# A two-layer block kernel: the second layer's middle norm taken from three sums, the residual added in pieces, and two transposed groups instead of six ahead of a product

## The chip, the cores and the metric

The kernel runs on one core of one Trainium2 chip. The metric is the device time of one execution in microseconds (us). Engines in the profile: PE is TensorE's matmul queue and PEld its weight loads, DVE is VectorE, ACT is ScalarE, POOL is GpSimd, SP is SyncE, which issues the weight transfers.

## What is computed

Two transformer layers over 256 tokens of width 2048. Only the second one matters here; in it the change touches the two places where an RMS norm stands ahead of a weight product. Cut to that:

```python
def rms_norm_2(x, g):
    y = x * lax.rsqrt(jnp.mean(x * x, axis=-1, keepdims=True) + EPS)
    return y * g

h = modulate(rms_norm_2(x, pre_norm_mix), shift_m, scale_m)   # first norm: ahead of w_in
...                                                           # attention on h @ w_in
o = jnp.concatenate([o_n, o_m], axis=-1) @ w_o
x = x + gate_m[:, None, :] * rms_norm_2(o, post_norm_mix)
h = modulate(rms_norm_2(x, pre_norm_ffn), shift_f, scale_f)   # middle norm: ahead of w_up
f = jnp.square(jax.nn.relu(h @ w_up)) @ w_down
```

Write g for `o * gate_m * post_norm gain` and r for the reciprocal root of the mean square of `o`. Then the new x is x + r g, and its mean square is mean(x²) + r (2 mean(x g) + r mean(g²)). That identity is what the changed kernel uses.

## The kernel before

Every weight product runs as a *phase* of *units*. A unit is a 512-row by 512-column piece of a weight matrix (`w_in2a` uses 432 columns); it is handled as two halves, and a half is 12 matmuls on PE: two blocks of 128 rows (kt), two blocks of 128 tokens (h), and three products each (high x high, high x low, low x high), since every fp32 operand is split in a high part and a remainder. A phase has two column blocks b of four units u; column block b accumulates in the PSUM banks `GP[:, 2b..2b+1]`. For each half ACT makes the high part (`whi`, `split_hi`) and DVE the remainder (`wlo`, `split_lo`) in a ring of four halves. `w_oa`, `w_ob` and some others also carry four *ada* units (DVE only, `ada_acc`), a matrix-vector product that makes the modulation vectors.

The left operand of a product behind a norm (`hhi`, `hlo`, transposed to 16 blocks of 128 features by 256 tokens) is made in eight groups g of two blocks. For one group: x times 1/rms goes into `xn` (`second_scale` on DVE for columns 0 to 511, `second_scaled(i, k)` on ACT for the later quarters k), PE transposes it (`second_turn`, eight matmuls on two groups, line 841), DVE applies gain and shift into one of two buffers `flat` (`second_full`, two instructions), ACT copies that to the high part (`second_upper`), DVE subtracts for the low part (`second_lower`, which releases semaphore `norm_lo`). Half (u, s) of column block 0 needs group 2u+s, and PE waits for it by `norm_lo`. i = 0 is the first norm, i = 1 the middle one. All queues are in program order; each engine's order is written out by hand, and *hooks* put small work behind a given unit of a phase, `{5: [...]}` behind the fifth unit.

Between `w_ob` and `up20`, in the kernel before: `post_mean` and `post_root` give r; DVE adds `x += r * g` in eight pieces of 512 columns (`post_add`, line 2231); ACT squares seven of them for the new mean square (line 1724), DVE the eighth (line 2250); a root; a reciprocal; then the scaling and the groups. PE transposes groups 0 to 5 ahead of the product, groups 6 and 7 behind its unit 0.

In `w_oa`, four small products `gate_row` on PE (line 1275) spread the gate vector over the partitions. They form a loop over engines: DVE makes a diagonal tile `dg` (line 2211) behind the two `wlo` of a unit, PE multiplies it behind the next unit, ACT copies the result (line 1682) and then makes the two `whi` of the next unit:

```python
phase(PH["w_oa"], joined(store(PH["w_oa"], o2), {3 + i: [lambda it, i=i: gate_copy(0, i)] for i in range(4)},
                         {7: [lambda it: post_block(0, 0)]}))
```

## Time and profile before

| what | value |
| --- | --- |
| runs | 2827.8, 2829.64, 2836.27 us; median 2829.64 us |
| profiled execution | 2827.76 us, its span 2825.9 us |
| PE busy | 2746.7 us, 97% of the span |
| PE weight loads busy | 2346.6 us, 83% |
| DVE busy | 1785.4 us, 63% |
| ACT busy | 1314.4 us, 47% |
| mean granted TensorE clock | 0.989 of full |

Busy time is the time in which an engine executed something; idle time of PE is where time can be won or lost in this kernel, while idle time of DVE and ACT costs nothing unless PE waits for them. The span is counted from the first to the last instruction; the remaining 1.9 us of the profiled execution lie around it.

### The profile page before, as it was taken

What the parts mean: (1) busy time and instruction counts of PE and PEld (TensorE: products, weight loads), DVE (VectorE), ACT (ScalarE), POOL (GpSimd) and SP (SyncE); (2) the same over time, 40 slices, a digit from 0 to 9 for tenths busy, and PEclk for the clock granted to TensorE, in tenths of its full rate; (3) what the DMA queues carried; (4) which work ended last, traced back from release to release, by engine and by line L of the source; (5) the groups of instructions that cost most, each with busy time, mean ns of one, the idle gap of its engine ahead of it and who ended that gap; (6) DMA issues with size and microseconds to landing.
All of it is one profiled execution on the core that took longest, in us unless ns stands there. A gap on an engine that the chain in (4) does not pass through costs nothing.

```text
span 2825.9 us, 34968 instructions
## 1 busy us (share of the span) xinstructions
PE 2746.7 (97%) x13414; PEld 2346.6 (83%) x13414; DVE 1785.4 (63%) x2030; ACT 1314.4 (47%) x1656; POOL 170.3 (6%) x132
## 2 busy tenths in 40 slices
PE   8998999999999999999999999998989999999998
PEld 8998888888778888888888889887878888888886
DVE  4466668776558888865555564546675756644555
ACT  5554244454435545434454554446454444344453
POOL 0001630000000000000000000820000000000000
PEclk9999999999999999999999999999999999999999
DMA  8553038887647777876556556550655866755553
GB/s 281 161 175 122 0 143 288 288 278 268 224 163 257 281 276 272 284 252 208 184 179 209 188 183 198 198 172 16 225 192 182 282 220 225 266 188 181 188 188 119
DMA packets 293266, 579.60 MB, mean 205 GB/s; under 512 B 9168, under 2 KB 46192, under 8 KB 292112
## 3 DMA queue, kind: packets, MB, share of 16 engines
q1 hardware_dynamic: 291296, 566.08, 59.6%
q0 software_dynamic: 1120, 8.57, 0.8%
q10 hardware_dynamic: 720, 3.15, 0.3%
q8 instruction: 90, 1.47, 0.2%
q14 instruction: 40, 0.33, 0.0%
HBM read 575.66 MB, written 2.10 MB: 204 GB/s over the span
## 4 chain that ended last, share of the span: by engine, by line
PE 94%; DVE 3%; ACT 1%; issue 1%; DMA 0%; POOL 0%; SPq 0%; DVEq 0%; ACTq 0%
PE GP L866 28%; PE GP L868 28%; PE GP L867 28%; PE TA L841 2%; PE TB L841 1%; PE TB L489 1%; PE GP L466 1%; PE TA L1225 0%; DVE x L2231 0%; PE GP L1069 0%; PE TA L1069 0%; PE GP L1059 0%; DVE wlo L1794 0%; DMA x<-in_x 0%; PE TA L1275 0%
## 5 line engine op out<-in xcount | busy, mean ns | idle before, releaser
L1794 DVE TENSOR_TENSOR wlo<-raw,whi 128x1024 fp32r<-128x1024 f32 (+2 forms) x904 | 1085.3, 1214 | 813.3 <-ACT whi L1318 804.1
L1318 ACT CAST whi<-raw 128x1024 fp32r<-128x1024 f32 (+2 forms) x904 | 923.7, 1029 | 1172.3 <-PE GP L868 1115.4
L866 PE MATMUL GP<-whi,hhi 128*128 128x512 f32 (+2 forms) x1792 | 688.6, 384 | 2.9 <-issue 2.9
L868 PE MATMUL GP<-whi,hlo 128*128 128x512 f32 (+2 forms) x1792 | 680.5, 380 | 0.0
L867 PE MATMUL GP<-wlo,hhi 128*128 128x512 f32 (+2 forms) x1792 | 679.9, 379 | 0.0
L866 PEld LDWEIGHTS GP<-whi,hhi 128*128 128x128 f32 x1792 | 337.6, 188 | 53.6 <-issue 4.4
L868 PEld LDWEIGHTS GP<-whi,hlo 128*128 128x128 f32 x1792 | 337.3, 188 | 52.2
L867 PEld LDWEIGHTS GP<-wlo,hhi 128*128 128x128 f32 x1792 | 337.7, 188 | 50.6 <-issue 1.0
L866 PE MATMUL GP<-whi,bhi 128*128 128x512 f32 x704 | 276.7, 393 | 0.2 <-DVE blo L1855 0.2
L1782 DVE SCALAR_TENSOR_TENSOR ada_acc<-raw,csig,ada_acc 128x512 f32<-128x512 f32 x360 | 270.2, 751 | 10.2
L868 PE MATMUL GP<-whi,blo 128*128 128x512 f32 x704 | 274.3, 390 | 0.0
L867 PE MATMUL GP<-wlo,bhi 128*128 128x512 f32 x704 | 273.9, 389 | 0.0
L866 PE MATMUL GP<-whi,f2hi 128*128 128x512 f32 x512 | 201.4, 393 | 0.0
L868 PE MATMUL GP<-whi,f2lo 128*128 128x512 f32 x512 | 199.3, 389 | 0.0
L867 PE MATMUL GP<-wlo,f2hi 128*128 128x512 f32 x512 | 199.3, 389 | 0.0
L868 PEld LDWEIGHTS GP<-whi,blo 128*128 128x128 f32 x704 | 132.1, 188 | 27.8
L866 PEld LDWEIGHTS GP<-whi,bhi 128*128 128x128 f32 x704 | 132.2, 188 | 27.2 <-DVE blo L1855 0.7
L867 PEld LDWEIGHTS GP<-wlo,bhi 128*128 128x128 f32 x704 | 132.3, 188 | 26.5
L866 PE MATMUL GP<-whi,fhi 128*128 128x512 f32 x352 | 137.3, 390 | 0.0
L868 PE MATMUL GP<-whi,flo 128*128 128x512 f32 x352 | 137.0, 389 | 0.0
L867 PE MATMUL GP<-wlo,fhi 128*128 128x512 f32 x352 | 136.9, 389 | 0.0
L867 PEld LDWEIGHTS GP<-wlo,f2hi 128*128 128x128 f32 x512 | 96.1, 188 | 20.7 <-issue 1.0
(416 smaller groups left out, 2601.2 us busy)
## 6 DMA issues: line engine op xcount, KB each, us to landing
raw<-in_w_up SPq DMA_DIRECT2D x108, 1024.0 KB, 5.3
raw<-in_w_down SPq DMA_DIRECT2D x108, 1024.0 KB, 5.1
raw<-in_w_ada SPq DMA_DIRECT2D x96, 1024.0 KB, 5.2
raw<-in_w_gate SPq DMA_DIRECT2D x44, 1024.0 KB, 5.3
raw<-in_w_in SPq DMA_DIRECT2D x48, 856.0 KB, 4.7
raw<-in_w_xkv SPq DMA_DIRECT2D x32, 1024.0 KB, 5.6
raw<-in_w_in SPq DMA_DIRECT2D x24, 1024.0 KB, 5.0
raw<-in_w_in SPq DMA_DIRECT2D x24, 864.0 KB, 4.6
```

What stands on the lines that cost most here:

```text
L466: m = pe.matmul(o[:, h * T:h * T + u["L"]], l, r, start=(d == 0), stop=(d == n - 1), skip_group_check=True)
L489: m = pe.matmul(bank[:, j * P:j * P + P], l, r, start=(d == 0), stop=(d == len(terms) - 1), skip_group_check=True)
L841: return pe.transpose(dst, src, ident[0:n, 0:n] if n != P else ident)
L866: pe.matmul(o, ahi[:, kt, t], whi[r][:, k, 0:q.width], start=first, stop=False)
L867: pe.matmul(o, ahi[:, kt, t], wlo[r][:, k, 0:q.width], start=False, stop=False)
L868: m = pe.matmul(o, alo[:, kt, t], whi[r][:, k, 0:q.width], start=False, stop=last)
L1318: nc.scalar.copy(whi[(2 * g + s) % NRING][:, :, 0:q.width], raw[j % NSLOT][:, 2 * s:2 * s + 2, 0:q.width])\
L1782: m = nc.vector.scalar_tensor_tensor(ada_acc[:, :], raw[j % NSLOT][:, k, :], c, ada_acc[:, :], ALU.mult, ALU.add)
L1794: TTo(wlo[r][:, :, 0:q.width], raw[j % NSLOT][:, 2 * s:2 * s + 2, 0:q.width], whi[r][:, :, 0:q.width].bitcast(F32), ALU.subtract).then_inc ...
```

## The change

Five edits:

1. In both norms PE transposes only groups 0 and 1 ahead of the product; groups 2 and 3, 4 and 5, 6 and 7 are transposed in the middle of units 0, 1 and 2 (behind their first half). ACT and DVE take the groups in an order to match.
2. The mean square of the new x comes from three sums of four blocks each. ACT squares x in `w_oa` (`x_squares`, eight instructions) and g in `w_ob` and behind it (`gated_squares`, eight); DVE multiplies x and g (`crossed`, eight), of which two instructions stand in `w_oa`, four in `w_ob` and two behind it.
3. The squares of the new x are gone: seven on ACT, one on DVE.
4. `x += r * g` is done in pieces: two `post_add` ahead of the scaling, the other six each between `second_full` and `second_lower` of groups 0 to 5 (`mixed_pair`). ACT scales quarter k of the new x only after both of its pieces.
5. Of the first quarter's two scalings in the middle norm ACT takes one and DVE the other.

```diff
-            for g in range(6):
+            for g in range(2):
                 second_turn(0, g)
             product(PH["w_in2a"], hhi, hlo, None, first=lambda: None, halves=lambda u, s: (S("norm_lo"), 32 + 2 * u + s + 1),
-                    points={(0, 0, 0): lambda: (second_turn(0, 6), second_turn(0, 7))})
+                    points=second_turns(0))
...
+            def second_turns(i):
+                return {(0, 0, u, "half"): lambda u=u: (second_turn(i, 2 * u + 2), second_turn(i, 2 * u + 3)) for u in range(3)}
...
+            def x_squares(b):
+                for h in range(NH):
...
+                    nc.scalar.activation(fbx[1], x[:, h, 512 * b:512 * b + 512], ACT.Square, scale=D ** -0.5,
+                                         accum_out=xs[:, 4 * h + b:4 * h + b + 1]).then_inc(S("x_ss"), 1)
...
             phase(PH["w_oa"], joined(store(PH["w_oa"], o2), {3 + i: [lambda it, i=i: gate_copy(0, i)] for i in range(4)},
+                                     {3 + b: [lambda it, b=b: x_squares(b)] for b in range(4)},
                                      {7: [lambda it: post_block(0, 0)]}))
...
-            for i in range(7):
-                b, h = divmod(i, 2)
-                act.wait_ge(S("y_mix"), i + 1)
-                act.wait_ge(S("norm_ss"), 31 + i)
-                nc.scalar.activation(junk[0][:, :], x[:, h, 512 * b:512 * b + 512], ACT.Square,
...
-            second_uppers(1)
+            second_scaled(1, 0)
+            second_upper(1, 0)
+            second_upper(1, 1)
+            second_scaled(1, 1)
+            split_hi(PH["up20"], 0, 1)
+            second_upper(1, 2)
+            second_upper(1, 3)
+            second_scaled(1, 2)
...
+            def crossed(b, h):
+                link(nc.vector.scalar_tensor_tensor(junk[1][:, :], o2[:, h, 512 * b:512 * b + 512], 2.0 / D, x[:, h, 512 * b:512 * b + 512],
+                                                    ALU.mult, ALU.mult, accum_out=xs[:, 8 + 4 * h + b:9 + 4 * h + b]))
+
+            def gated_sums(b):
+                gated(0, b).then_inc(S("og"), 1)
+                dve.wait_ge(S("og"), b + 1)
+                for h in range(NH):
+                    crossed(b, h)
...
-            second_pair(1, 0)
+
+            def mixed_pair(b):
+                for h in range(NH):
+                    second_full(1, 2 * b - 2 + h)
+                    post_add(0, b, h, "y_mix")
+                    second_lower(1, 2 * b - 2 + h)
+
+            mixed_pair(1)
             split_lo(PH["up20"], 0, 1)
-            second_pair(1, 2)
-            second_pair(1, 4)
+            mixed_pair(2)
...
-                phase(PH[f"up2{s}"], hooks, head={3: [] if s else [lambda it: second_pair(1, 6)]})
+                phase(PH[f"up2{s}"], hooks, head={3: []} if s else {3: [lambda it: mixed_pair(3)], 4: [lambda it: second_pair(1, 6)]})
```

What stands on DVE behind the scaling of the middle norm, before. `flat<-TA` and its like are `second_full`, `hlo<-` is `second_lower`, `wlo<-` is `split_lo` of `up20`; the words in brackets are the semaphores that an instruction waits for.

```order
L2142 TENSOR_SCALAR flat<-TA,tab,shifts 128x256 [waits norm_lo,norm_t]
L2142 TENSOR_SCALAR flat<-TA,tab,shifts 128x256
L2142 TENSOR_SCALAR flat<-TA,tab,shifts 128x256 [waits norm_lo,norm_t]
L2142 TENSOR_SCALAR flat<-TA,tab,shifts 128x256
L2149 TENSOR_TENSOR hlo<-flat,hhi 128x512 [waits norm_hi] x2
L1794 TENSOR_TENSOR wlo_55<-raw,whi_51 128x1024 [waits hi_done]
L1794 TENSOR_TENSOR wlo_56<-raw,whi_52 128x1024 [waits hi_done]
L2142 TENSOR_SCALAR flat<-TB,tab,shifts 128x256 [waits norm_lo,norm_t]
```

The same place in the changed kernel, up to the same instruction; `x<-o` is `post_add`:

```order
L2173 TENSOR_SCALAR flat<-TA,tab,shifts 128x256 [waits norm_lo,norm_t]
L2173 TENSOR_SCALAR flat<-TA,tab,shifts 128x256
L2262 SCALAR_TENSOR_TENSOR x<-o_50_110,small,x 128x512
L2180 TENSOR_TENSOR hlo<-flat,hhi 128x512 [waits norm_hi]
L2173 TENSOR_SCALAR flat<-TA,tab,shifts 128x256 [waits norm_lo,norm_t]
L2173 TENSOR_SCALAR flat<-TA,tab,shifts 128x256
L2262 SCALAR_TENSOR_TENSOR x<-o_50_110,small,x 128x512
L2180 TENSOR_TENSOR hlo<-flat,hhi 128x512 [waits norm_hi]
L1825 TENSOR_TENSOR wlo_55<-raw,whi_51 128x1024 [waits hi_done]
L1825 TENSOR_TENSOR wlo_56<-raw,whi_52 128x1024 [waits hi_done]
L2173 TENSOR_SCALAR flat<-TB,tab,shifts 128x256 [waits norm_lo,norm_t]
```

Each group now carries one piece of the residual between its full values and its low part.

On ACT at the same place, in the changed kernel (`xn_p<-x` is `second_scaled`, `hhi<-flat` is `second_upper`, `whi<-raw` is `split_hi` of `up20`):

```order
L1630 CAST hhi<-flat 128x512 [waits norm_f] x2
L1625 ACTIVATE xn_p_113<-x,small 128x512 [waits y_mix]
L1625 ACTIVATE xn_p_113<-x,small 128x512
L1327 CAST whi_51<-raw 128x1024 [waits mm_done,raw_in1]
L1327 CAST whi_52<-raw 128x1024 [waits mm_done]
L1630 CAST hhi<-flat 128x512 [waits norm_f] x2
```

Before, quarters 1 and 2 were scaled ahead of all of this, and the two casts of `raw` stood directly behind the first two of `hhi`.

On ACT in `w_oa`, in the changed kernel, a stretch of the loop through `gate_row`; the row with `flat,small<-x` is new:

```order
L1690 COPY gpb_51_111<-TA 128x512 [waits gate_mm]
L1719 ACTIVATE flat,small<-x 128x512 [waits x_ss] x2
L1327 CAST whi_49<-raw 128x1024 [waits mm_done,raw_in2]
L1327 CAST whi_50<-raw 128x1024 [waits mm_done]
L1690 COPY gpb_51_111<-TA 128x512 [waits gate_mm]
```

The two squares stand between the copy of a gate row and the casts of the next unit; before, the casts followed the copy directly.

## Rows read from the trace of the kernel before

**Rows 1.** Whom PE waited for: us in total, times, longest us

```profile
PE TA L841 <- DVE xn_p L2132: 11.3, 1, 11.3
```

**Rows 2.** Timeline of PE, middle norm: start us, us, instruction [idle before <- releaser]

```profile
2089.18 1.97 PE L841 MATMUL TA<-cst,xn_p 128*128 128x128 f32 x8 [11.26 <-DVE xn_p L2132]
...
2094.05 0.48 PE L866 MATMUL GP<-whi,hhi 128*128 128x512 f32 x1
...
2099.99 1.09 PE L841 MATMUL TA<-cst,xn_p 128*128 128x128 f32 x8 [0.25 <-ACT xn_p L1614]
2100.84 0.47 PE L866 MATMUL GP<-whi,hhi 128*128 128x512 f32 x1
```

**Rows 3.** Timeline of DVE, middle norm

```profile
2078.31 0.69 DVE L2239 TENSOR_TENSOR o<-GP,gpb 128x512 f32<-128x512 f32 x1 [2.80 <-ACT junk L1689]
...
2080.62 5.39 DVE L2231 SCALAR_TENSOR_TENSOR x<-o,small,x 128x512 f32<-128x512 f32 x8
2086.04 0.69 DVE L2250 SCALAR_TENSOR_TENSOR junk<-x 128x512 f32<-128x512 f32 x1
...
2086.78 0.17 DVE L2091 TENSOR_TENSOR shifts<-mod,tab 128x16 f32<-128x16 f32 x1
...
2088.24 0.88 DVE L2132 TENSOR_SCALAR xn_p<-x,small 128x512 f32<-128x512 f32 x2
2090.33 1.90 DVE L2142 TENSOR_SCALAR flat<-TA,tab,shifts 128x256 f32<-128x256 f32 x4 [1.21 <-PE TA L841]
2092.15 1.46 DVE L2149 TENSOR_TENSOR hlo<-flat,hhi 128x512 fp32r<-128x512 f32 x2
2093.87 2.36 DVE L1794 TENSOR_TENSOR wlo<-raw,whi 128x1024 fp32r<-128x1024 f32 x2 [0.25 <-ACT whi L1318]
```

**Rows 4.** Timeline of ACT, middle norm

```profile
2088.24 2.56 ACT L1614 ACTIVATE xn_p<-x,small 128x512 f32<-128x512 f32 x4 [0.23 <-DVE small L2256]
2091.36 0.62 ACT L1619 CAST hhi<-flat 128x512 fp32r<-128x512 f32 x1 [0.56 <-DVE flat L2142]
...
2092.80 1.99 ACT L1318 CAST whi<-raw 128x1024 fp32r<-128x1024 f32 x2
```

**Rows 5.** Timeline of PE, first norm

```profile
1642.19 1.97 PE L841 MATMUL TA<-cst,xn_f 128*128 128x128 f32 x8 [6.02 <-DVE xn_f L2132]
...
1646.98 0.44 PE L866 MATMUL GP<-whi,hhi 128*128 128x432 f32 x1
...
1653.17 0.44 PE L866 MATMUL GP<-whi,hhi 128*128 128x432 f32 x1
```

**Rows 6.** Timeline of DVE, first norm

```profile
1645.16 1.46 DVE L2149 TENSOR_TENSOR hlo<-flat,hhi 128x512 fp32r<-128x512 f32 x2
```

**Rows 7.** Timeline of PE, second and third gate row in `w_oa`

```profile
2003.40 1.02 PE L1275 MATMUL TA<-dg,cst 128*128 128x512 f32 x2
...
2009.75 1.02 PE L1275 MATMUL TA<-dg,cst 128*128 128x512 f32 x2
```

**Rows 8.** Timeline of ACT in `w_oa`

```profile
2004.94 2.00 ACT L1318 CAST whi<-raw 128x1024 fp32r<-128x1024 f32 x2
...
2019.54 0.63 ACT L1689 ACTIVATE junk<-o 128x512 f32<-128x512 f32 x1
...
2020.92 1.03 ACT L1318 CAST whi<-raw 128x1024 fp32r<-128x1024 f32 x1
```

**Rows 9.** Timeline of DVE in `w_oa`

```profile
2008.38 0.68 DVE L2211 TENSOR_TENSOR dg<-cst,mod 128x512 f32<-128x512 f32 x1
```

**Rows 10.** Stretches: length, busy time (instructions) by engine, granted clock, DMA share, GB/s

```profile
301.20:308.60 7.40, 6.74 (x32) 6.06 (x32) 7.40 (x9) 0.59 (x1) 3.80 (x3) 0.55 0.00 0
2089.10:2093.80 4.70, 4.62 (x22) 4.62 (x23) 3.21 (x7) 3.85 (x7) 0.00 (x0) 0.50 0.01 2
1958.20:1962.00 3.80, 1.42 (x7) 1.42 (x8) 3.59 (x10) 2.81 (x12) 0.00 (x0) 0.84 0.02 4
...
2045.00:2056.00 11.00, 11.00 (x50) 9.10 (x49) 8.87 (x9) 4.33 (x5) 0.00 (x0) 1.00 0.75 244
```

More of the change, by code:

```diff
@@ L869, in iteration @@
                             m.then_inc(S("mm_done"), 1)
+                            if s == 0 and isinstance(it, int) and (it, b, u, "half") in points:
+                                points[it, b, u, "half"]()
                         if mid and b % 2 == 1 and u == 1:
@@ L1280, in _ @@
             product(PH["w_ob"], hhi, hlo, lambda u: N("natt", "lo", 8))
-            for g in range(6):
+            for g in range(2):
                 second_turn(1, g)
@@ L1612, in second_scaled @@
                 X, xn, r = seconds[i][0:3]
-                for h in range(NH):
+                if i:
+                    act.wait_ge(S("y_mix"), 2 * k + 2 if k else 1)
+                for h in range(NH if k else 1):
                     m = nc.scalar.activation(xn[:, h, 512 * k:512 * k + 512], X[:, h, 512 * k:512 * k + 512], ACT.Copy, scale=r[:, h:h + 1])
@@ L2130, in second_scale @@
                 X, xn, r = seconds[i][0:3]
-                for h in range(NH):
+                for h in range(i, NH):
                     m = nc.vector.tensor_scalar(xn[:, h, 0:512], X[:, h, 0:512], r[:, h:h + 1], None, ALU.mult)
@@ L2231, in post_add, with x_means @@
                 nc.vector.scalar_tensor_tensor(x[:, h, c], osq[n][:, h, c], ors[:, h:h + 1], x[:, h, c], ALU.mult, ALU.add).then_inc(S(done), 1)
-            phase(PH["w_oa"], {3 + i: [lambda it, i=i: gate_column(0, 32, i)] for i in range(4)} | {8: [lambda it: gated(0, 0)]}, links=2)
+            def crossed(b, h):
[6 more added lines that the diff above has]
+                    crossed(b, h)
+            def x_means(it):
+                dve.wait_ge(S("x_ss"), 8)
+                link(nc.vector.tensor_reduce(xsum, xs[:, 0:8].rearrange("p (a b) -> p a b", b=4), AX.X, ALU.add))
+                link(nc.vector.tensor_scalar(xt[:, 0:2], xsum, EPS, None, ALU.add))
+            phase(PH["w_oa"], {3 + i: [lambda it, i=i: gate_column(0, 32, i)] for i in range(4)} | {8: [lambda it: gated_sums(0)]}, links=2)
             c3 = slice(1536, 2048)
@@ L2237, in last_columns @@
                 dve.wait_ge(S("mm_done"), block_end(PH["w_ob"], 0, 1) + NRING)
+                TTo(o2[:, 0, c3], GP[:, 2, :], gpb[0][:, c3], ALU.mult).then_inc(S("og"), 1)
                 dve.wait_ge(S("norm_ss"), 30)
[L2239 to L2243 removed]
@@ L2244, in _ @@
-            dve.wait_ge(S("evac1"), 1 + PH["w_ob"].ev1)
-            post_scale(0)
-            for b in range(4):
-                for h in range(NH):
-                    post_add(0, b, h, "y_mix")
-            dve.wait_ge(S("y_mix"), 8)
-            link(nc.vector.scalar_tensor_tensor(junk[1][:, :], x[:, 1, c3], 1.0, x[:, 1, c3], ALU.mult, ALU.mult, accum_out=beta[:, 15:16]))
-            modulation(1, 48, 5)
-            dve.wait_ge(S("norm_ss"), 38)
-            link(nc.vector.tensor_reduce(xsum, beta[:, 8:16].rearrange("p (a b) -> p a b", b=4), AX.X, ALU.add))
@@ L2254, in _ @@
-            nc.vector.tensor_scalar(xmean, xsum, 1.0 / D, EPS, ALU.mult, ALU.add).then_inc(S("norm_ms"), 1)
+                TTo(o2[:, 1, c3], GP[:, 3, :], gpb[0][:, c3], ALU.mult).then_inc(S("og"), 1)
+            phase(PH["w_ob"], {3: [x_means], 4: [lambda it: gated_sums(1)], 8: [lambda it: gated_sums(2)], 10: [last_columns]}, lead=1)
+            post_mean(0)
+            dve.wait_ge(S("og"), 5)
+            dve.sem_inc(S("evac1"), 1)
+            crossed(3, 0)
+            crossed(3, 1)
+            post_scale(0)
```

78 lines of the change are left out of this document (50 added, 28 removed).

## The prediction

> **What bounds the kernel now.** I read the page first: PE is busy for 97% of the span, and the chain of work that ended last lies on it almost throughout, so only PE's idle time and the work that is added to its queue count. The view of whom PE waited for has the new scaled x of the middle norm as its longest wait, 11.3 us [rows 1]. The timeline of PE there shows it whole: the last product of `w_ob` ends at about 2077.5, transposing starts at 2089.18, the product of `up20` at 2094.05, and it stops once more, for the transposes of groups 6 and 7 [rows 2]. The first norm has a wait of 6.0 us and the same form [rows 5]. Then I read DVE and ACT in the same stretches for what fills the wait and what each piece costs [rows 3, 4, 6], the loop through the gate rows, since the change puts work into it [rows 7 to 9], and the granted clock around PE's waits [rows 10]. The reader is to see that an end at which PE starts the product earlier is worth something only if groups 2 to 7 then come as fast as PE wants them.
>
> **Prices.** Start to start, from [rows 3, 4]: the full values of a group, two instructions, 0.91 us (four in 1.82); its low part 0.69; a residual piece 0.67 (eight in 5.39), some 0.07 more to its end; a product with a sum (line 2250, the form of `crossed`) 0.74; a `wlo` 1.14 (two in 2.36 to the end); on ACT a scaling 0.64, a `hhi` 0.62, and a pair of `whi` 2.0, the first done after 1.05. Two halves of `up20` fill PE from 2094.05 to its stop 0.25 ahead of 2099.99, and 0.24 of that is the end of the last matmul: 2.72 us a half. Eight transposes take 1.76 at the low clock and 0.85 at the high one [rows 2]: the same eight instructions, ahead of the product and behind its unit 0.
>
> **The middle norm, start.** Before, DVE came to its first residual piece at 2080.62. In the changed kernel its first product on GP needn't wait for ACT's square (it begins at 2078.31 only because of that wait): 0.6 less. Ahead of the first piece now stand two `crossed` (1.5), the three small modulation instructions (0.62, as from 2086.78 on) and the sum's reduction and five small ones, 0.85 at the same 0.2 for each that waits for the one before: the first piece starts at 2080.62 - 0.6 + 1.5 + 0.6 + 0.85 = 2083.0. Meanwhile ACT does one more square between, which is over by 2081. Two pieces, a reciprocal hidden between them, and one scaling of 0.5: PE starts transposing at 2085.1, 4.1 us earlier. DVE reads the first group 1.15 us after that start, as before, at 2086.2. Then a row of the new order is: full values 0.91, piece, low part. The low part waits for `hhi`, which begins 1.03 after the full values and takes 0.62; so a row is 1.69 + 0.69 = 2.4 us, and the piece costs its time, as `hhi` alone would have been in reach only 0.1 later. The first low part is there at 2088.6, and the product starts at 2088.65 instead of 2094.05: **5.4 us earlier**. It is the whole gain.
>
> **The middle norm, afterwards.** Behind the two rows of a `mixed_pair` come two `wlo`, and those wait for ACT, which first scales the next quarter, and may do so only after the pair's second piece. From the start of a pair: second piece done at 2.4 + 0.91 + 0.75 = 4.05; two scalings 1.35; first cast 1.05; first `wlo` starts at 6.5; two of them: the next pair starts at **8.8**. PE wants 6.3 for the same (two halves and eight transposes). Before, DVE did groups 2 to 5 without a piece, without waiting for a scaling, and with one pair of `wlo` less among them. So low part 2 comes at 2097.4, low part 4 at 2106.2. The last pair, which carries no piece, has both full values ahead of its low parts: the third cycle ends at 2112.55, plus 1.82 and 0.69: low part 6 comes at 2115.1. PE, which would be through with the half before at 2095.0 (or at about 2097.5, if the clock is still low), at 2104.1 and at 2112.8, waits for each. In the kernel before the same half, the seventh, began at 2100.84 + 4 x 2.72 = 2111.7. From there on the two are alike: **3.4 us later, net**. The low clock costs nothing here, since DVE is last. Bounds: if the waits for casts are half hidden (0.9 per cycle, three cycles) it is +0.7; if the clock falls again in the waits, +5.
>
> **The first norm.** Nothing ahead of PE's start at 1642.19 changes. The product starts when the first low part is there, 1645.16 + 0.69, so at 1645.9 instead of 1646.98 [rows 5, 6]. Groups 2 to 5 now cost PE 2 x 0.85 inside the product that were spent ahead of it. A narrower half is 2.36 (two of them, eight transposes and 0.6 of waiting make the 6.19 between the last two rows). Half 4 waits 0.9 for its group: group 2 is transposed behind half 0, from 1648.3; DVE has it 0.6 later and is through with groups 2 and 3 at 1652.1; ACT, done with their `hhi` at 1651.3, scales until 1652.6 and casts until 1653.5; two `wlo` of 0.97, two full values and a low part end at 1657.95, where PE is at 1657.05. Half 6 then starts at 1645.9 + 6 x 2.36 + 3 x 0.85 + 0.9 = 1663.5. Before it was 1653.17 + 4 x 2.36 = 1662.6. That is +0.9 at the high clock. But PE now stops for 1.9 us between two transposed groups and the product. Before, PE worked from its start without a stop and had the high clock after about 4.7 us (in rows 10 the stretch from 2089.10 has 0.50 to its end; the same in the first norm). Where it worked with a short stop, from 301.2 on, it had the low clock, save for the first 0.7 us, until about 308.7, 7.5 us after its start [rows 10]. So the high clock comes back between 1646.9 and 1649.7, and the first half, begun at 1645.9, loses 0.5 to 1.9 us, and 2.3 if it all runs at 1.2 GHz. I take 1.8, near the row with a stop. **+2.7 us**, between +1.4 and +3.2.
>
> The stretch from 2089.10 holds nothing but transposes, and the clock was high behind it. The Trainium skill (TensorE: Matmul & The Clock Gate, Part 4: PE-mode transpose) says that the full clock isn't engaged for the transpose mode, since it doesn't count as PE work in the same way. By that rule the clock would come back only with the product's own work, the first half would run low to its end, and the first norm would be at +3.2 instead of +2.7; the trace doesn't bear it out (rival e).
>
> **The gate rows of `w_oa`.** A loop: a gate row starts on PE; ACT copies it and casts the next unit from 1.54 us after that start; DVE's two `wlo` follow, then `dg`, which ends at 2008.38 + 0.68 = 2009.06, 5.66 after the start at 2003.40. PE wants it 6.35 after the start, at 2009.75: 0.7 to spare [rows 7 to 9]. The change puts two squares on ACT between copy and casts. Two such squares take 2020.92 - 2019.54 = 1.4 [rows 8]. The loop becomes 7.05, and PE waits 0.7 at the second, third and fourth gate row: **+2.1 us**. The squares behind the fourth row are in front of nothing that PE waits for at once. Bounds: 0 (the loop has more room than the semaphores show) and 3.
>
> **What costs nothing.** The four `crossed` in `w_ob` and the two in `w_oa` (0.75 each) lie in DVE's idle time: in the stretch from 2045 to 2056 DVE is busy 8.9 of 11 us with the ada unit and a `gated` in it, and ACT 4.3 [rows 10], and there are halves in the ring ahead of PE (the low part of half 8 would be done at about 2054.2, wanted at 2055.4). If that cover were gone, each pair would cost up to 1.5. The gated squares lie in ACT's idle time there. Queued behind the delayed ada units are only slots of the weight ring, whose transfers SP issues 1.5 us later; they are wanted several us after landing. The removed seven squares of ACT are part of the start's gain already.
>
> **The sum.** -5.4 + 8.8 = +3.4, +2.7, +2.1: **+8.2 us**. Against the profiled execution's 2827.76 that is 2836.0; the median of the runs shown is 1.9 above that execution, so 2837.8.
>
> **The rivals.** (a) *The groups keep up.* If DVE and ACT overlap as they did before, the middle norm is worth -5.4 + 1.7 (the transposes of groups 2 to 5 within the product) = -3.7; with +0.9 and no other cost it is about -3 us, 2827. For it speaks that PE waited only 0.25 us at its later stop before; against it that the pieces, which filled 4 us ahead of the start, now stand in the chain of the groups. The point from which it decides is a cycle of 6.3 us on DVE. Even this isn't faster by 0.3%. Chance 0.12. (b) *The gate rows stay free.* The squares hide and the rest holds: +6, 2836. Chance 0.15. (c) *The clock falls in PE's waits*, and the time ends on the other side. In the middle norm PE now waits about 2 us three times, and between 1958.20 and 1962.00, where PE stood still for 2.4 us, the mean clock is 0.84, so it fell [rows 10]. At 1.2 instead of 2.4 GHz a half of 2.72 costs 5.4; where DVE is last that hides, but behind half 6 it doesn't. One fall that counts is +2.7, so 11 us and 2840.5. It decides if one of the waits is as long as that standstill. Chance 0.25. (d) The forecast, with all three terms: 0.40. (e) *Transposes don't bring the clock back*: the first half all at the low clock, 0.5 more, 8.7 us and 2838.3; the stretch from 2089.10 speaks against it [rows 10]. Chance 0.08.
>
> **How the numbers follow.** About 0.3%, 8.5 us, is what a measurement of this kernel can tell from no change. My sum of 8.2 lies just inside. Slower: half of (d) and of (e) and three quarters of (c), 0.43. Within: the other halves, the rest of (c), (b), and half of (a), 0.51. Faster: half of (a), 0.06, and it would need a gain besides that no row shows. The range goes from (a)'s upper side, 2829, to (c) with the upper bounds of the gate rows and the first norm, 8.2 + 2.7 + 1.4 = +12.3, and the runs' own spread of some 3 us: 2845.
>
> **What would show it.** In the changed profile: PE starts transposing for the middle norm about 7.6 us after the last product of `w_ob`, and `up20` 11.1 after it, against 16.5. Then three waits of PE within `up20` for `hlo`, each of about 2 us (the first shorter if the clock is low), with DVE's pairs 8.8 apart and DVE idle for 1.8 behind each, released by `whi`. In the first norm the first half at the low clock and a wait of about 1 us for group 4. In `w_oa` three waits of 0.7 for `dg`. The forecast is wrong if DVE's cycle is below 7 us, if PE isn't idle ahead of the gate rows, or if a wait turns up in `w_ob`.

## The result and the profile of the changed kernel

| | before | changed |
|---|---|---|
| median of 20 runs each, us | 2828.97 | 2837.73 |
| lowest to highest, us | 2826.98 to 2839.16 | 2835.01 to 2840.13 |
| profiled execution: span (time), us | 2825.9 (2827.76) | 2837.5 (2839.28) |

The changed kernel takes 1.0023 times as long, 95% interval [1.0015, 1.003]: by the ratio some 4 to 8.5 us more, by the medians 8.8. By the ratio it is inside the 0.3% that the prediction counted as no change. The forecast was 2837.8. (One run of the kernel before, in the comparison of the kernels "middle norm filled" and "pieces left out" below, took 4152.34 us with a granted clock of 0.63 over the whole run; the ratios leave it out.) Whom PE waited for in the changed kernel (us in total, times, longest); the row for `xn_p` answers to [rows 1].

```profile
PE TA L842 <- DVE xn_p L2163: 7.5, 1, 7.5
PE GP L867 <- issue: 6.3, 4, 1.8
PE TA L842 <- DVE xn_f L2163: 6.0, 1, 6.0
...
PE GP L867 <- DVE hlo L2180: 3.0, 3, 1.8
PE TA L1284 <- DVE dg L2242: 1.9, 4, 0.6
```

The wait of 11.3 us is down to 7.5, and two kinds of wait have grown: for low parts (`hlo`) inside the products, of which the kernel before had none, and for `dg`, of which it had one of 0.3. The row with `issue` is time for which the view names no releaser; it was 2.9 us before. Two of its stops, 1.79 and 1.66 us, are those between PE's two transposed groups and the product; in the middle norm the first low part is done at 2096.68 + 0.69 = 2097.37, and the product starts at 2097.47. The timeline of PE in the middle norm, against [rows 2], says where (columns: start us, us, instruction, idle before and its releaser):

```profile
2093.84 1.97 PE L842 MATMUL TA<-cst,xn_p 128*128 128x128 f32 x8 [7.52 <-DVE xn_p L2163]
...
2097.47 0.77 PE L867 MATMUL GP<-whi,hhi 128*128 128x512 f32 x1 [1.66 <-issue]
...
2098.89 0.63 PE L867 MATMUL GP<-whi,hhi 128*128 128x512 f32 x1
...
2100.17 0.63 PE L867 MATMUL GP<-whi,hhi 128*128 128x512 f32 x1
...
2102.37 0.60 PE L842 MATMUL TB<-cst,xn_p 128*128 128x128 f32 x4
...
2114.55 0.50 PE L867 MATMUL GP<-whi,hhi 128*128 128x512 f32 x1 [1.77 <-DVE hlo L2180]
...
2116.39 0.63 PE L867 MATMUL GP<-whi,hhi 128*128 128x512 f32 x1
...
2117.67 0.63 PE L867 MATMUL GP<-whi,hhi 128*128 128x512 f32 x1
...
2123.22 0.50 PE L867 MATMUL GP<-whi,hhi 128*128 128x512 f32 x1 [0.44 <-DVE hlo L2180]
```

Line 867 comes once for every three products. Spaced 1.28 us in the first half (2098.89 to 2100.17) it is at 1.2 GHz (granted clock 0.50 from 2098.89 to 2101.45); at 2.4 GHz the spacing is 0.68. The half from 2114.55 on, behind a wait of 1.77, falls to 1.28 as well. DVE and ACT in one cycle, against [rows 3, 4]:

```profile
2095.00 1.00 DVE L2173 TENSOR_SCALAR flat<-TA,tab,shifts 128x256 f32<-128x256 f32 x2 [1.21 <-PE TA L842]
2095.91 0.75 DVE L2262 SCALAR_TENSOR_TENSOR x<-o,small,x 128x512 f32<-128x512 f32 x1
2096.68 0.69 DVE L2180 TENSOR_TENSOR hlo<-flat,hhi 128x512 fp32r<-128x512 f32 x1
...
2101.28 2.36 DVE L1825 TENSOR_TENSOR wlo<-raw,whi 128x1024 fp32r<-128x1024 f32 x2 [1.62 <-ACT whi L1327]
2103.55 0.99 DVE L2173 TENSOR_SCALAR flat<-TB,tab,shifts 128x256 f32<-128x256 f32 x2
```

```profile
2098.31 0.62 ACT L1630 CAST hhi<-flat 128x512 fp32r<-128x512 f32 x1 [1.67 <-DVE flat L2173]
2098.97 1.34 ACT L1625 ACTIVATE xn_p<-x,small 128x512 f32<-128x512 f32 x2
2100.21 1.98 ACT L1327 CAST whi<-raw 128x1024 fp32r<-128x1024 f32 x2
```

The pairs start at 2095.00, 2103.55, 2112.12 and 2120.68: 8.56 apart, with DVE idle for 1.62 in each while ACT scales and casts. Last, PE in the first norm [rows 5] and at the gate rows [rows 7]:

```profile
1645.63 1.97 PE L842 MATMUL TA<-cst,xn_f 128*128 128x128 f32 x8 [6.02 <-DVE xn_f L2163]
1649.38 0.70 PE L867 MATMUL GP<-whi,hhi 128*128 128x432 f32 x1 [1.79 <-issue]
...
1653.84 1.05 PE L842 MATMUL TB<-cst,xn_f 128*128 128x128 f32 x4
1654.69 0.66 PE L842 MATMUL GP<-cst,xn_f 128*128 128x128 f32 x4
...
1657.54 0.41 PE L867 MATMUL GP<-whi,hhi 128*128 128x432 f32 x1
...
1664.06 0.46 PE L867 MATMUL GP<-whi,hhi 128*128 128x432 f32 x1 [0.74 <-DVE hlo L2180]
...
2003.07 1.02 PE L1284 MATMUL TA<-dg,cst 128*128 128x512 f32 x2
...
2010.09 1.12 PE L1284 MATMUL TA<-dg,cst 128*128 128x512 f32 x2 [0.51 <-DVE dg L2242]
...
2017.28 1.12 PE L1284 MATMUL TA<-dg,cst 128*128 128x512 f32 x2 [0.58 <-DVE dg L2242]
```

**Reading by stretches.** The time between two instructions of PE that every kernel has tells more here than the whole, since the clock in stages that no edit touches moves the whole by some us. Five stretches are used from here on, four with edits in them and one without: the first norm (from its first transposes to the first of the 15-row `p` in the attention), the attention (from there to the first product of `w_oa`; no edit touches it), `w_oa` (from its first product to the first transposes of the first ada unit), `w_ob` (from there to the same of the second), and the middle norm (from there to the first transposes of `tok` in `up20`). In us, with the median of the whole run; "over" is the median's distance to the kernel before in the same comparison:

| kernel | first norm | attention | `w_oa` | `w_ob` | middle norm | median | over |
|---|---|---|---|---|---|---|---|
| before | 275.93 | 67.97 | 47.24 | 43.99 | 50.84 | 2828.97 | |
| changed | 279.61 | 66.83 | 49.66 | 43.99 | 54.00 | 2837.73 | 8.8 |
| first norm as before | 275.91 | 66.81 | 49.63 | 43.98 | 53.98 | 2833.93 | 5.0 |
| squares ahead of the copy | 279.61 | 69.01 | 47.28 | 44.02 | 53.97 | 2835.93 | 7.0 |
| casts in the gaps | 279.59 | 66.83 | 49.63 | 43.99 | 50.81 | 2837.19 | 8.3 |
| first norm filled | 277.54 | 73.36 | 49.66 | 44.01 | 55.62 | 2843.49 | 14.6 |
| middle norm filled | 279.34 | 66.82 | 49.63 | 43.99 | 53.94 | 2836.95 | 9.1 |
| pieces left out | 279.01 | 66.81 | 49.61 | 43.98 | 53.55 | 2838.94 | 11.0 |
| three edits | 275.90 | 66.82 | 47.27 | 43.99 | 50.27 | 2827.87 | -1.1 |
| four turns | 276.56 | 67.99 | 47.26 | 44.00 | 50.97 | 2830.87 | 1.9 |
| three edits, middle filled | 275.92 | 71.25 | 47.27 | 43.99 | 48.87 | 2829.37 | 0.4 |
| waits filled | 275.42 | 66.79 | 47.28 | 43.99 | 48.41 | 2827.15 | -2.1 |

In the two profiled executions the changed kernel is 11.6 us longer. 3.7 + 2.4 + 0.0 + 3.2 = 9.3 lie in the four stretches with edits. 3.4 arose ahead of the first norm, in stages that no edit touches, and 1.1 was won back in the attention. Those two are not of the change. By the starts of the same instructions the 3.4 is made up of 1.1 won by 262 us, 1.6 lost from there to 311 us, nothing worth naming to 760 us, and 3.0 lost from there to 802 us. In the last of these the same 64 products (`kTx` by `qTx`) took 16.37 us instead of 14.08, with a granted clock of 0.63 from 759 to 765 us and of 0.77 to 770 us, where the kernel before had 1.00. The granted clock of the changed kernel in the earlier one of the two (columns as in rows 10):

```profile
262.00:264.00 2.00, 1.23 (x8) 1.13 (x7) 2.00 (x1) 0.00 (x0) 2.00 (x1) 0.54 0.00 0
264.00:274.00 10.00, 8.71 (x30) 6.05 (x31) 1.65 (x2) 6.07 (x9) 0.14 (x1) 0.58 0.00 0
...
278.00:286.00 8.00, 4.50 (x20) 4.17 (x21) 7.79 (x11) 3.08 (x3) 0.00 (x0) 0.58 0.00 0
```

The kernel before had 1.00, 0.66 and 0.79 in the same three stretches, with the same instructions. Such a difference belongs to one execution and not to a kernel: the unedited attention takes 66.8 to 73.4 us in the table.

### The profile page after: what moved, and what is told of

It is laid out like the page before. It is cut to its first block, busy times and chain, and to the rows that moved or that the text cites. A ratio compares the mean times of both kernels' runs of the same rounds, so it can differ in the third digit from the quotient of the medians.

```text
span 2837.5 us, 35015 instructions
## 1 busy us (share of the span) xinstructions
PE 2755.1 (97%) x13414; PEld 2349.1 (83%) x13414; DVE 1791.6 (63%) x2049; ACT 1322.2 (47%) x1675; POOL 171.0 (6%) x132
## 4 chain that ended last, share of the span: by engine, by line
PE 93%; DVE 4%; ACT 2%; issue 1%; DMA 0%; POOL 0%; SPq 0%; DVEq 0%; ACTq 0%
PE GP L867 28%; PE GP L869 28%; PE GP L868 28%; PE TA L842 2%; PE TB L842 1%; PE TB L490 1%; PE GP L467 1%; DVE wlo L1825 1%; PE TA L1234 0%; DVE flat L2173 0%; ACT whi L1327 0%; PE GP L1072 0%; PE TA L1072 0%; PE GP L1062 0%; DVE x L2262 0%
```

## The experiments

**Each term undone by itself.** The first kernel puts the first norm back:

```diff
-            for g in range(2):
+            for g in range(6):
                 second_turn(0, g)
...
-                    points=second_turns(0))
+                    points={(0, 0, 0): lambda: (second_turn(0, 6), second_turn(0, 7))})
...
             second_pair(0, 2)
+            second_pair(0, 4)
```

(and ACT's `second_scaled` and `second_upper` of index 0, and DVE's `final_x`, in the order of before).

> The changed kernel with the first norm put back to six transposed groups ahead of the product; everything else stays. If the price of the first norm is what its stretch in the changed profile shows (from the start of its transposes to the start of w_oa 346.4 us against 343.9 before, +2.5), this run has 343.9 +- 0.3 there and is 2.5 us faster than the changed kernel as a whole; the gate rows and the middle norm keep their costs. Rival: the first norm's price is an accident of where the clock happened to rise, then the stretch stays near 346 or scatters by a us or more.

Measured 2833.93 us (2830.6 to 2846.42, 11 runs), ratio to before 1.0027 [1.0016, 1.0039]. The first norm takes 275.91, as before; the other stretches stay as changed. So the edit of the first norm costs 3.7 us in this profile, and 3.7 to 3.8 by the medians. The expectation's own mark missed: it ran from the transposes to the start of `w_oa`, said 343.9 +- 0.3, and came to 342.72, since it includes the unedited attention (66.81 here, 67.97 in the kernel before). Against the changed kernel's 346.44 that is 3.7 as well, not the 2.5 that was expected; the table's shorter stretch leaves the attention out for this reason.

```diff
-            phase(PH["w_oa"], joined(..., {3 + i: gate_copy(0, i)}, {3 + b: x_squares(b)}, ...
+            phase(PH["w_oa"], joined(..., {3 + b: x_squares(b)}, {3 + i: gate_copy(0, i)}, ...
```

> The changed kernel with the two squares of x on ACT in each hook of w_oa ahead of the copy of the gate row instead of behind it, in the 3.9 us in which ACT waits for that row. If the loop through the gate rows is what costs (w_oa from its first matmul to the transposes of its ada sum 49.66 us against 47.24 before), the three waits of PE for dg (0.51, 0.58, 0.55) are gone, the stretch is 47.2 to 47.4 and the kernel is 2.4 us faster than the changed one. Rival: the squares cost through something that doesn't depend on their place (slower casts beside them, more reads of the same memory), then the stretch stays over 48.5.

Measured 2835.93 us (2832.33 to 2839.88, 8 runs), ratio 1.0023 [1.0012, 1.0033]. The second to fourth gate rows are again 6.35 apart and have no idle time ahead of them, and `w_oa` takes 47.28. The whole is 1.8 us nearer to the kernel before, where 2.4 were expected, with runs that spread over 7 us. The squares fit into ACT's idle time ahead of the gate row; behind its copy they lay in the loop.

```profile
2006.05 1.02 PE L1284 MATMUL TA<-dg,cst 128*128 128x512 f32 x2
...
2012.40 1.02 PE L1284 MATMUL TA<-dg,cst 128*128 128x512 f32 x2
```

The third takes the casts of `up20`'s first units out of the chain of the groups: the first unit is cast while DVE makes the three sums, the second and third each in two parts, between `hhi` casts.

```diff
             gated_squares(3, (1,))
+            split_hi(PH["up20"], 0, 1)
             act.wait_ge(S("norm_ms"), 7)
...
             second_scaled(1, 1)
-            split_hi(PH["up20"], 0, 1)
+            split_hi(PH["up20"], 0, 2, (0,))
             second_upper(1, 2)
+            split_hi(PH["up20"], 0, 2, (1,))
             second_upper(1, 3)
             second_scaled(1, 2)
+            split_hi(PH["up20"], 0, 3, (0,))
...
```

> The changed kernel, in the middle norm ACT casts the weights of up20's units 1 to 3 in its idle gaps ahead of the uppers of each group instead of behind the scaling; DVE's order stays. Theory: DVE's pairs are 8.6 us apart because its wlo wait 1.62 for those casts. They then follow at once, the pairs are 7.0 apart, PE's waits for hlo (1.77 and 0.44) go, and the middle norm is bound by PE itself: half 6 of up20 starts about 3 us earlier, the whole about 3 us faster than the changed kernel. Rival: DVE's own work or the wait for a transpose sets the distance, then the pairs stay over 8 us apart and the gain is under 1 us.

Measured 2837.19 us (2832.15 to 2840.01, 7 runs), ratio 1.0024 [1.001, 1.0038]. The median alone, only 0.5 under the changed kernel's where 3 was expected, tells nothing with this scatter; the stretch does: 50.81 against 54.00. DVE's pairs start 8.0, 7.7 and 6.9 us apart, the two `wlo` follow the low part without a wait, and PE waits 0.2 in front of halves 4 and 6:

```profile
2100.11 0.69 DVE L2185 TENSOR_TENSOR hlo<-flat,hhi 128x512 fp32r<-128x512 f32 x1
2100.72 2.35 DVE L1830 TENSOR_TENSOR wlo<-raw,whi 128x1024 fp32r<-128x1024 f32 x2
2104.17 1.00 DVE L2178 TENSOR_SCALAR flat<-TB,tab,shifts 128x256 f32<-128x256 f32 x2 [1.10 <-PE TB L842]
```

But 50.81 is only what the kernel before had. Now DVE waits for PE, whose first half is still at the low clock.

**The low clock.** Eight transposes more, whose results nobody reads, fill PE's stop of 1.8 us in the first norm:

```diff
             for g in range(2):
                 second_turn(0, g)
+            pe.wait_ge(S("p2_x"), 1)
+            for k in range(8):
+                turn(TB[:, (k % 4) * P:(k % 4) * P + P], xn_f[:, k % 2, (4 + k // 2) * P:(5 + k // 2) * P])
```

> The changed kernel with eight more transposes, whose result nothing reads, in the first norm between the two transposed groups and the product, where PE stood still for 1.79 us. It tests what brought the clock back. If PE's standing still kept it low and transposes count as work, it is back about 4.7 us after the first transpose as before the change, the first half runs mostly at the high clock, and the stretch to the start of w_oa is 1 to 2 us shorter (344.5 to 345.4 against 346.4). If transposes don't count (the rule on the transpose mode), the first half runs at the low clock as in the changed kernel and the stretch stays at 346.4 or more.

The timeline of PE in that kernel:

```profile
1642.69 1.97 PE L842 MATMUL TA<-cst,xn_f 128*128 128x128 f32 x8 [6.02 <-DVE xn_f L2166]
1644.45 1.91 PE L842 MATMUL TB<-cst,xn_f 128*128 128x128 f32 x8
1646.44 0.70 PE L867 MATMUL GP<-whi,hhi 128*128 128x432 f32 x1
...
1647.54 0.35 PE L867 MATMUL GP<-whi,hhi 128*128 128x432 f32 x1
...
1648.11 0.36 PE L867 MATMUL GP<-whi,hhi 128*128 128x432 f32 x1
```

The product starts 3.75 us after the transposes, as in the changed kernel, but the high clock is back 4.7 to 4.8 us after PE's start, where with the stop it took 9.1 (1645.63 to 1654.69, in the rows above). The stretch is 2.07 shorter: that is the price of the low clock in the first norm. The whole, however, measured 2843.49 us (2840.14 to 2846.04, 5 runs), ratio 1.0051 [1.0037, 1.0065], which neither theory had: the attention took 73.4 us against 66.8 in the changed kernel, with a granted clock of 0.66 from 1920 to 1930, where the changed kernel in the same work had 1.00, and the middle norm 1.6 more. So the expectation's mark, up to the start of `w_oa`, came to 350.9, outside of both theories. That nothing in those stages was edited is sure; why their clock fell is open. The filling can't be the only thing that brings it about: the kernel of the three edits with only its middle norm filled, whose first norm is that of the kernel before, has 71.25 in the attention.

The same filling in the middle norm alone:

```diff
             for g in range(2):
                 second_turn(1, g)
+            for k in range(7):
+                turn(TB[:, (k % 4) * P:(k % 4) * P + P], xn_p[:, k % 2, (k // 2) * P:(1 + k // 2) * P])
```

> The changed kernel with seven more transposes of the scaled first quarter, whose results nobody reads, between PE's two transposed groups and the product of up20: PE has no stop of 1.7 us there, and the first half should run at the high clock, as it did with the same filling in the first norm (2.1 us gained there). Theory A (DVE's chain is last in the middle norm): the first half ends 2 us sooner, but PE then waits those 2 us longer for the low part of group 2; from the last ada unit to the first tok transposes 54.0 us as in the changed kernel, and the whole within 1 us of it, so some 8.5 us over the kernel before. Theory B (the low clock of the first half is what the middle norm lost): 51.8 us for the stretch, and 2 us less in the whole.

```profile
2095.20 0.76 PE L867 MATMUL GP<-whi,hhi 128*128 128x512 f32 x1 [0.16 <-issue]
...
2103.71 0.50 PE L867 MATMUL GP<-whi,hhi 128*128 128x512 f32 x1 [1.54 <-DVE hlo L2182]
...
2112.27 0.50 PE L867 MATMUL GP<-whi,hhi 128*128 128x512 f32 x1 [1.78 <-DVE hlo L2182]
```

Measured 2836.95 us (2836.77 to 2843.0, 5 runs), ratio 1.0037 [1.0023, 1.0052], stretch 53.94 against 54.00. Theory A holds: a first half that takes 3.2 us instead of 4.9 (turns behind it at 2098.40, not shown) turns into a wait of 1.54 for group 2's low part, which the changed kernel did not have. The low clock cost the middle norm nothing while DVE's chain was last.

**What sets DVE's cycle.** Six of the eight residual pieces are left out, so x is not brought up to date in three of its quarters:

```diff
                     second_full(1, 2 * b - 2 + h)
-                    post_add(0, b, h, "y_mix")
+                    dve.sem_inc(S("y_mix"), 1)
                     second_lower(1, 2 * b - 2 + h)
```

> The changed kernel, with six of the eight residual pieces of the middle norm left out (x keeps its old values in the last three quarters, only the semaphore is counted), so DVE has 6 x 0.75 us less to do. Theory A (the cycle of DVE's pairs is set by ACT: the second group's hhi, two scalings, then the casts): hhi of the second group still ends 3.9 us after the pair's start, the cycle stays at 8.5 us, the stretch at 53.9, and the time changes by less than 0.5 us; the pieces were free there. Theory B (the pieces, put into the chain of the groups, cost their own time): a cycle of 7.1 us and 3 to 4 us less.

```profile
2094.79 1.00 DVE L2173 TENSOR_SCALAR flat<-TA,tab,shifts 128x256 f32<-128x256 f32 x2 [1.21 <-PE TA L842]
2096.47 0.69 DVE L2180 TENSOR_TENSOR hlo<-flat,hhi 128x512 fp32r<-128x512 f32 x1 [0.68 <-ACT hhi L1630]
...
2100.93 2.36 DVE L1825 TENSOR_TENSOR wlo<-raw,whi 128x1024 fp32r<-128x1024 f32 x2 [1.48 <-ACT whi L1327]
2103.21 0.99 DVE L2173 TENSOR_SCALAR flat<-TB,tab,shifts 128x256 f32<-128x256 f32 x2
```

Measured 2838.94 us (2833.65 to 2841.9, 5 runs), ratio 1.0037 [1.0023, 1.0051]. The cycle goes from 8.56 to 8.42, not to 7.1: 0.68 of idle time stands where each piece was, released by `hhi`. The stretch is 53.55, and the whole is 1 to 2 us over the changed kernel, where a change under 0.5 was expected; with five runs that spread over 8 us this says nothing. The cycle and the stretch bear out theory A. The pieces lie behind the casts of `hhi` almost for nothing, 0.07 each; the cycle is set by the chain that goes through ACT: full values, `hhi`, scalings, first cast, then the two `wlo`.

**The three edits together** (the first three diffs of this section in one kernel), and what they lead to:

> The changed kernel with three edits together: the first norm with six groups turned ahead, as before; the squares of x ahead of ACT's copy of the gate row; the casts of the middle norm put into ACT's gaps. Theory A (the change's loss is the sum of three terms that have nothing to do with each other, 3.7 + 2.4 + 3.2 = 9.3 us): stretches as in the kernel before (275.9 from the first turns to the attention's, 47.3 for w_oa, 50.8 for the middle norm) and the whole within 1.5 us of the kernel before, so the new mean square wins nothing even then. Theory B (part of the loss comes from elsewhere, or the edits get in each other's way): 3 us or more above the kernel before.

Measured 2827.87 us (2827.01 to 2839.12, 12 runs) against 2828.95 (29 runs), ratio 1.0001 [0.9988, 1.0013]. Every stretch with edits is as before or under it; 9.9 us less than the changed kernel by the medians, where the three terms make 9.3. The loss is accounted for. The 50.27 of the middle norm is partly luck: the same code gave 50.81 with the casts alone moved and 50.97 with four turns, and the high clock was back 6.9 us after PE's start here, 8.2 and 8.5 there.

The next one keeps the edits of `w_oa` and of the middle norm, and has four groups turned ahead in the first norm:

```diff
-            for g in range(2):
+            for g in range(4):
                 second_turn(0, g)
...
-                    points=second_turns(0))
+                    points={at: turns for at, turns in second_turns(0).items() if at[2]})
```

> As the kernel of the three edits, but the first norm has four groups turned ahead of the product, where the kernel before has six and the changed one two: PE's stop of 1.8 us between turns and product is filled with useful turns. Theory A (the first norm's 3.7 us are mostly the low clock of the first half, 2.1 as the filled kernel showed, and the turns inside the product): from the first turns to the attention's 276.9 us, 1.0 over before and 2.7 under the changed kernel; the whole 1 us over the kernel of the three edits. Theory B (the turns of groups 4 to 7 inside the product hold up the low parts as well): 278 us.

Measured 2830.87 us (2827.38 to 2834.76, 12 runs), ratio 1.0001 [0.9989, 1.0013]. The first norm takes 276.56, 0.63 over before: theory A, a little better than its 1.0. The whole is 3.0 over the kernel of the three edits by the medians, where 1 was expected; 1.2 of it lies in the attention of the two profiles and 0.7 in the middle norm, which have the same code in both. Two groups more ahead of the product cost nothing, since PE had to stop there, and they give back 3 us.

Then the seven filling transposes of the middle norm, by the same lines as above, on top of the three edits:

> The kernel of the three edits with seven more transposes of the scaled first quarter, whose results nobody reads, between PE's two transposed groups of the middle norm and the product of up20, so that PE has no stop of 1.7 us there. In this kernel ACT's casts wait for PE's use of the ring, so a first half at the high clock moves everything behind it. Theory A: 1.1 us of the 2.4 that the low clock takes come through (DVE reads group 2 at once after its two wlo instead of 1.1 later): stretch 49.7, the whole 1 us under the kernel of the three edits and about 0.5 to 1 us under the kernel before. Theory B: DVE's own work of 6.8 to 7 us per pair is last, stretch 50.6, no gain.

```profile
2098.50 0.47 PE L867 MATMUL GP<-whi,hhi 128*128 128x512 f32 x1 [0.39 <-issue]
...
2101.40 0.66 PE L842 MATMUL TB<-cst,xn_p 128*128 128x128 f32 x4
```

Measured 2829.37 us (2825.31 to 2835.85, 12 runs), ratio 0.9995 [0.9983, 1.0007]. The stretch is 48.87: 1.4 to 2.1 less than in the three profiles without the filling, 2.0 less than before. Theory A, which had said 49.7, is nearer than B. The excess over its 1.1 is in part luck: the high clock was back only 2.9 us after PE's start, earlier than in any other profile here. The first half takes 2.9 us (2098.50 to 2101.40), and with the casts out of the chain that is felt. The whole was to be 1 us under the kernel of the three edits; its median is 1.5 over it, inside the scatter.

Last, both long waits are filled too; ahead of the first norm's turns stand the same two lines with 48:

```diff
+            for k in range(60):
+                turn(TA[:, (k % 4) * P:(k % 4) * P + P], ident)
             for g in range(2):
                 second_turn(1, g)
```

> The kernel of the three edits with the filled middle norm, and PE's two long waits filled as well: 48 transposes of the identity ahead of the first norm's turns (6.0 us of waiting) and 60 ahead of the middle norm's (7.5 us), whose results nobody reads. Theory A (what is left of the low clock there is the turns themselves, 1.97 against 1.09 us for eight, of which DVE, which reads after the first four, feels 0.5): from the first turns to the attention's 275.4, the middle norm 48.4 from the last ada unit to the first tok transposes, and the whole 1 us under the kernel filled only in the middle. Theory B (PE that is kept busy here shows a low clock somewhere later, as in the kernel that was filled in the first norm, whose attention took 6 us more): the stretches are shorter, but the whole is some us longer than without.

```profile
2076.38 6.71 PE L842 MATMUL TA<-cst 128*128 128x128 f32 x60
2084.06 1.09 PE L842 MATMUL TA<-cst,xn_p 128*128 128x128 f32 x8 [0.97 <-DVE xn_p L2172]
...
2087.23 0.47 PE L867 MATMUL GP<-whi,hhi 128*128 128x512 f32 x1 [1.31 <-issue]
```

Measured 2827.15 us (2822.17 to 2831.64, 12 runs) against 2829.26, ratio 0.9992 [0.9981, 1.0002]. Both stretches come out as theory A said (275.42 and 48.41), and the attention has 66.79, the shortest in the table, so theory B's low clock did not turn up in the profiled execution, whose span of 2822.1 is the shortest of all profiled ones. It is the best kernel found, 2.1 us under before by the medians, but its interval still includes 1: a gain of 0.1% is likely, not shown. Nor does it show what the three sums are worth: no run fills the long waits of the kernel before. There the first low part was done at 2092.15 + 0.69 = 2092.84 [rows 3] and the product started at 2094.05, behind transposes at the low clock, so filling alone might win 1.2 us or more in its middle norm; this is an estimate.

## Why the prediction was right, and where it was off

**The time** was forecast at 2837.8 and came to 2837.73. That close a hit owes something to chance: the sum of 8.2 was 1.1 too small against the 9.3 of the stretches; the median before that it stood on was 0.7 too high, and the medians lie only 8.8 apart.

**The first norm, forecast +2.7, bounds +1.4 to +3.2: measured +3.7** in the changed kernel's profile (3.1 and 3.4 in the profiles of the kernels with the pieces left out and with the middle norm filled, which have the same first norm). It is the term that was sized wrong, and the only one outside its bounds. The product began 3.75 us after the transposes (forecast 3.7), the wait for group 4 was 0.74 (0.9), the turns inside the product cost what was said at the high clock. Off is "I take 1.8" for the low clock, with the upper bound of 2.3: from 1649.38 to 1653.84 the half took 4.46 instead of 2.36, and the first turns behind it ran low too (1.27 for eight, against 0.79 for the next eight), so 2.6 in all. The row with a stop had the clock back 7.5 us after PE's start; here it took 9.1, and in four other kernels with this first norm 9.1, 9.2, 8.6 and 7.9, with stretches of 279.59, 279.61, 279.34 and 279.01: how much the term costs hangs on when the clock rises, and differs from one execution to the next. The bound had been cut to the half itself. The first product of each half also takes some 0.08 longer than the others.

**The gate rows, +2.1: measured +2.4.** The loop came to 7.1 us (2010.09 to 2017.28 is 7.19, forecast 7.05), with three waits of 0.51, 0.58 and 0.55; a part of the rest is PE's slower start behind each wait (the gate row itself 1.12 instead of 1.02). The mechanism is shown by the experiment that only swaps the order of the squares and the copy. Rival (b) is refuted.

**`w_ob` and what costs nothing: 0, measured 0.00.**

**The middle norm, +3.4: measured +3.2**, from errors that cancel. The start was 0.4 worse: transposing 3.7 us earlier and not 4.1, the product 5.0 and not 5.4. From the product on GP to the first piece it took 5.8 (2085.92 to 2091.72), where 5.3 had been worked out. From the end of the last product of `w_ob` (2085.89) it is 8.0 us to the transposes and 11.6 to `up20`, where the forecast said 7.6 and 11.1. The cycle was 8.56, not 8.8, three times. There ACT's scaling starts with the end of the second `hhi` (2098.31 + 0.62), 3.97 after the pair's start, and the two come 0.1 faster than the sum had them. The sentence "the piece costs its time" is wrong, though the row's length was nearly right: a row takes 2.29 us with the piece (2095.00 to 2097.29) and 2.29 without it (2094.79 to 2097.08), since DVE then waits 0.68 for `hhi`. Only 0.07 of each 0.75 comes through, at ACT's scaling, which waits for the second piece. "The low clock costs nothing here, since DVE is last" is shown by the filled kernel, and also that it stops being true once the casts are moved. The first of "three waits of about 2 us" was hidden in full by the slow half, as the text allowed; the third came to 0.44.

**The third wait was short because of rival (c).** The clock did fall, in the half behind the wait at 2114.55, where the granted clock over the half is 0.62. The half took 4.4 us, and DVE used them: the fall hid, and the wait behind it shrank from some 2 to 0.44. In the kernel with the pieces left out the clock did not fall, and there the third wait is 1.90. The condition set for (c), a fall behind half 6, did not come about in this execution. The stretch was 53.9 to 54.0 in the profiles of four kernels with this chain; in that of the fifth, the filled first norm, it was 55.6, and there the condition came about, in half 6:

```profile
2124.82 0.50 PE L867 MATMUL GP<-whi,hhi 128*128 128x512 f32 x1 [1.90 <-DVE hlo L2183]
...
2125.93 0.63 PE L867 MATMUL GP<-whi,hhi 128*128 128x512 f32 x1
...
2127.21 0.63 PE L867 MATMUL GP<-whi,hhi 128*128 128x512 f32 x1
```

The fall cost the 1.6 us by which the stretch is longer, not the 2.7 that (c) had for it, since the clock was back before the next half. So (c) is a matter of the single execution: in the same code the fall hid four times and counted once.

**Rival (a)**, that groups keep up, needed a cycle of 6.3; it was 8.56. With the casts moved the three cycles were 8.0, 7.7 and 6.9, and the middle norm was then worth 0, and not -3.7, mostly since PE's first half was slow. **Rival (e)**, that transposes don't bring the clock back: the filled first norm had the high clock back 4.8 us after its first transpose, after sixteen transposes and two products, and in the kernel before it came back 4.7 us after 2089.18, with nothing but transposes behind it [rows 2, 10]. Sixty transposes of the identity held the high clock by themselves, 6.71 us for 60, with the eight behind them at 1.09 instead of 1.97. The Trainium skill (TensorE: Matmul & The Clock Gate, Part 4: PE-mode transpose) says that the full clock isn't engaged for the transpose mode; the trace does not agree. Rival (e)'s time, 2838.3, is 0.6 from the result, and its +3.2 for the first norm is nearer to the measured 3.7 than the +2.7 of the forecast: the first half did run low to its end, but behind a stop of PE. The filled kernel differs from the changed one only in what PE does in that stop, so these rows, and not the time, tell the two apart.

**Where did the gain go?** The three sums do what they are for: 3.7 us of the wait vanish, and the product starts 5.0 earlier. It is given back inside `up20`: 1.6 for the turns of four groups that used to lie in the wait, and 6.5 in waits and slow halves, with cycles of 8.56 against the 6.3 that PE wants. With the casts moved, the second part falls to 3.4, most of it the first half's low clock. With PE filled too, 2.0 of 5.0 stay, in the execution whose clock rose early.

## What to carry to other kernels

A product that starts earlier gains only what its next operands can follow: work out the cycle of the engine that makes them (here full values, `hhi`, scaling, casts, `wlo`), and take out of it what another buffer would allow earlier, here the weight casts. Work that PE does while it would wait anyway is free and keeps its clock; moving it into the product costs it once in full and, where it leaves a stop of PE in the low clock, once more in clock. Where single us matter, compare the stretch between two marks in the trace rather than whole times, whose runs spread over 12 us in the kernel before and 5 us in the changed one, and look at the clock in a stretch before its last half us is believed.

## What the runs showed of the hardware

- A short stop of PE in the low clock delays the high clock, mostly by more than itself. With a stop of 1.7 to 1.8 us between the first eight transposes and the product it came back 6.9 to 9.4 us after PE's start (13 such starts in the profiles of nine kernels); without the stop after 2.9 to 5.7 us (9 starts in seven kernels). The same code differs by up to 1.6 us in this from one execution to the next.
- fp32 transposes alone brought the high clock back (kernel before, 4.7 us after 2089.18), and held it (waits filled, 60 in 6.71 us at a granted clock of 1.00).
- Waits of 1.5 to 1.9 us in the middle norm let the clock fall in some executions and not in others: about 1 us behind the wait of 1.77 at 2114.55 in the changed kernel, and not at all behind waits of 1.72 and 1.90 in the kernel with the pieces left out.
- The same code got a different clock from one execution to the next in stages in which PE has many short waits: at 262 to 286 us (granted 0.58 against 0.66 and 0.79 for the same instructions), at 760 to 802 us (0.84 against 0.92, 3.0 us of the two profiles' difference), and in the attention (66.8 to 73.4 us for the same instructions).
- Filling a stop at 1646 us went with a low clock in the attention at 1920 us in its profile, and with all five of its runs above 2840. The kernel with both waits filled did not show it, and a kernel without filling in the first norm had 71.25 us in the attention. Whether the two are linked is not settled.
